# RWKV pair of a two-layer hybrid trunk: second head's products in the other two quarters of TensorE, and a new order of the work ahead

## The reference

```python
r, k, v = heads(xr @ w_rkv[0]), heads(xk @ w_rkv[1]), heads(xv @ w_rkv[2])
g = sigmoid(xg @ g1) @ g2
kk = l2_normalize(k * k_k)
logw = -softplus(-heads(w0[d] + tanh(xw @ w1[d]) @ w2[d])) - 0.5
a = sigmoid(heads(a0[d] + (xa @ a1[d]) @ a2[d]))
kd = k * (1 + (a - 1) * k_a)
# scan over tokens, context first, then latent
sa = S @ a_t
S = S * w_t + sa b_t^T + v_t k_t^T
y_t = S @ r_t
```

## Time and profile before

| | |
|---|---|
| time before, median of 3 runs | 2366.2 us (2364.81 to 2370.7) |
| the profiled execution | 2360.81 us |
| its span | 2359.0 us |
| TensorE busy | 2285.1 us, 97% |
| VectorE busy | 1561.0 us, 66% |
| ScalarE busy | 1271.2 us, 54% |
| instructions | 57897 |

### The profile page before, as it was taken

The page is one execution under the profiler, slowest core; times in us unless marked ns, Lnnn a source line. Parts: engine busy times, 40 slices in busy tenths (PEclk is TensorE's granted clock), DMA queues, the critical chain, the costliest instruction groups (busy, mean ns, idle before and its releaser), DMA issues.

```text
span 2359.0 us, 57897 instructions
## 1 busy us (share of the span) xinstructions
PE 2285.1 (97%) x25130; PEld 1898.5 (80%) x25130; DVE 1561.0 (66%) x1768; ACT 1271.2 (54%) x1407; POOL 217.8 (9%) x208
## 2 busy tenths in 40 slices
PE   8999999999999889999998899999999999999998
PEld 5677566888888478888888788888888888888886
DVE  2544785322332766556666278888888888888888
ACT  4322024322222655555554277878777878777874
POOL 2000551000000041111112020000000000000010
PEclk9999999999999999999999999999999999999999
DMA  8466225333322521111102489999999999999994
GB/s 290 183 219 246 71 80 171 89 89 97 99 89 93 166 63 60 60 60 60 51 24 65 173 323 368 373 374 370 374 367 381 361 374 370 380 360 384 357 392 172
DMA packets 228493, 512.00 MB, mean 217 GB/s; under 512 B 15271, under 2 KB 108223, under 8 KB 228031
## 3 DMA queue, kind: packets, MB, share of 16 engines
q1 hardware_dynamic: 225470, 498.61, 58.3%
q10 hardware_dynamic: 1730, 7.10, 0.9%
q0 software_dynamic: 1152, 4.19, 0.6%
HBM read 492.58 MB, written 17.30 MB: 216 GB/s over the span
## 4 chain that ended last, share of the span: by engine, by line
PE 93%; DVE 3%; issue 1%; ACT 1%; DMA 1%; POOL 0%; ACTq 0%; DVEq 0%
PE bank L1700 27%; PE bank L1730 13%; PE bank L1205 3%; PE bank L1206 3%; PE bank L1207 3%; PE bank L1332 2%; PE bank L1111 2%; PE bank L1364 2%; PE bank L1082 2%; PE bank L1083 2%; PE bank L1084 2%; PE bank L1375 2%; PE bank L1223 2%; PE bank L1222 2%; PE bank L1224 2%
## 5 line engine op out<-in xcount | busy, mean ns | idle before, releaser
L3100 DVE TENSOR_TENSOR w_low<-expert_w,w_high 128x1792 fp32r<-128x1792 f32 (+2 forms) x384 | 771.8, 2024 | 121.4 <-ACT w_high L2250 118.5
L2250 ACT CAST w_high<-expert_w 128x1792 fp32r<-128x1792 f32 (+2 forms) x384 | 652.1, 1701 | 217.2 <-PE bank L1700 144.7
L1700 PE MATMUL bank<-w_high,xg_high 128*128 128x448 f32 x1024 | 294.3, 369 | 4.2 <-DVE xg_low L3090 4.2
L1700 PE MATMUL bank<-w_low,xg_high 128*128 128x448 f32 x1024 | 293.2, 368 | 0.0
L1700 PE MATMUL bank<-w_high,xg_low 128*128 128x448 f32 x1024 | 293.1, 367 | 0.0
L1700 PEld LDWEIGHTS bank<-w_high,xg_high 128*128 128x128 f32 x1024 | 191.6, 189 | 21.6 <-DVE xg_low L3090 4.4
L1700 PEld LDWEIGHTS bank<-w_high,xg_low 128*128 128x128 f32 x1024 | 192.8, 188 | 16.9
L1700 PEld LDWEIGHTS bank<-w_low,xg_high 128*128 128x128 f32 x1024 | 193.1, 189 | 15.8
L1730 PE MATMUL bank<-w_high,hid_high 128*128 128x512 f32 x448 | 175.8, 392 | 0.0
L1730 PE MATMUL bank<-w_high,hid_low 128*128 128x512 f32 x448 | 174.9, 390 | 0.0
L1730 PE MATMUL bank<-w_low,hid_high 128*128 128x512 f32 x448 | 174.7, 390 | 0.0
(11 more groups left out here) (440 smaller groups left out, 4109.3 us busy)
## 6 DMA issues: line engine op xcount, KB each, us to landing
expert_w<-in_moe_w_dram SPq DMA_DIRECT2D x128, 1792.0 KB, 9.6
expert_w<-in_moe_w_dram SPq DMA_DIRECT2D x32, 2048.0 KB, 10.3
arena<-in_mod_w_dram SPq DMA_DIRECT2D x48, 1024.0 KB, 8.6
expert_w<-in_moe_w_dram SPq DMA_DIRECT2D x32, 1536.0 KB, 10.0
arena<-in_ffn_w_dram SPq DMA_DIRECT2D x44, 512.0 KB, 5.1
slot_rows<-arena SPq DMA_DIRECT2D x25, 512.0 KB, 5.5
arena<-in_hy_w_in_dram SPq DMA_DIRECT2D x12, 1024.0 KB, 5.3
arena<-in_rw_w_rkv_dram SPq DMA_DIRECT2D x48, 256.0 KB, 2.8
```

Source lines behind the costliest of these rows:

```text
L1700: last = pe.matmul(bank[b0 + v][:, 0:EH], x[:, k, :], w_[:, kk, v * EH:v * EH + EH], start=(k == 0 and x is XGH and w_ is wh), stop=(k == ...
L2250: act.copy(high_piece(kind, n), piece(kind, ering[q % ERN], n // 2, n % 2))\
L3100: dve.tensor_tensor(piece(kind, low[s], n // 2, n % 2), piece(kind, ering[s], n // 2, n % 2), high_piece(kind, n).bitcast(F32), ALU.subtract)\
```

## The change

- z: one step for both heads, in which for each chunk matrix head 1 uses (0,0) and (1,1) and head 2 the quarters (0,1) and (1,0).
- wu: head 2 likewise; the loop runs over d, then b, then both heads, and waits once, for both inverses. Its four sums are in banks 2d + h. The steps and copies are ordered by direction first.
- For that, head 2's matrices have their halves exchanged: `scored` writes them so (`flip`), and a is turned in pieces: per chunk matrix a transpose of 64 rows to 128 columns for head 1, and for head 2 a 64x64 product with the identity and a 64x64 transpose. ScalarE copies a by head, not by direction.
- Decay and rate of direction 0 stay ahead of wu, those of direction 1 move behind it, on TensorE and on ScalarE (behind the four copies of wu).
- VectorE adds the last level into the inverse before the bonus, not after it.
- The values of the next pair go to bank 2, from bank 6, the queries to bank 3, from bank 7. Value tile 0 stands before m, tile 1 between m and n, tile 2 behind the local output products, tiles 3 to 7 in the scan, one per state. For the pairs after the first, tiles 0 to 2 are one product of 512 columns rather than four of 128; so is the key sum.
- The local output moves into the upper halves of the banks of g (0 and 1), and `g_sum` is signalled behind it; the output projection uses banks 2, 3, 6, 7.
- PAIR_FILL becomes 4 and stands behind the queries.

```diff
-PAIR_FILL, FIRST_FILL = 3, 4
+PAIR_FILL, FIRST_FILL = 4, 4
...
-            return bank[(0, 1, 6, 7)[m // 2]][:, m % 2 * SEQ:m % 2 * SEQ + SEQ]
+            return bank[(2, 3, 6, 7)[m // 2]][:, m % 2 * SEQ:m % 2 * SEQ + SEQ]
...
-                if d == 0:
-                    fill(PAIR_FILL)
...
-                for t in range(NB):
-                    cs = slice(t * P, t * P + P)
-                    last = mm(bank[0][:, cs], heads1, KS[:, cs], start=True, stop=True)
-                last.then_inc(sem("ahead_products"), one("ahead_products", "key_sum"))
+                mm(bank[0][:, :], heads1, KS, start=True, stop=True)\
+                    .then_inc(sem("ahead_products"), one("ahead_products", "key_sum"))
...
-                    step(pe, "ahead_copies", "rate_sig_1", j)
-                    step(pe, "pair_vectors", "n_ready_1", j - 1)
+                    step(pe, "pair_copies", "wu_copy_01", j - 1)
+                    if isinstance(j, int) and j == 0:
+                        pe.wait_ge(sem("lora_taken"), 4)
                 for k in tiles:
-                    for t in range(NB):
-                        cs = slice(t * P, t * P + P)
-                        last = mm(bank[6][:, cs], wst[:, 2, k, :], XV[:, k, cs], start=(k == 0 and t == 0), stop=(k == KT - 1),
+                    width = T if j and k < 3 else P
+                    for t in range(T // width):
+                        cs = slice(t * width, t * width + width)
+                        last = mm(bank[2][:, cs], wst[:, 2, k, :], XV[:, k, cs], start=(k == 0 and t == 0), stop=(k == KT - 1),
...
                 step(pe, "pair_vectors", "g_ready_1", i - 1)
-                settle(pe)
-                scores("scored", 0, At, Bt)
                 step(pe, "pair_copies", "out_copy", i - 1)
                 settle(pe)
-                scores("keys_scored", 2, Kt, At)
+                scores("scored", 0, At, Bt, 1)
+                step(pe, "ahead_copies", "query_copy", i)
+                settle(pe)
+                scores("keys_scored", 2, Kt, At, 0)
...
-                def z(h):
-                    if h == 0:
-                        step(pe, "pair_copies", "v_copy", i)
+                def z():
+                    step(pe, "pair_copies", "v_copy", i)
                     settle(pe)
                     for x in range(2 * NB):
-                        for s_ in range(2):
-                            last = mm(bank[6 + h][hd(s_), x * C:x * C + C], AakT[h][hd(s_), x, :],
-                                      Vt[hd(s_), x % NB, hd(h)], start=True, stop=True)
-                    last.then_inc(sem("pair_products"), one("pair_products", f"z_{h}"))
+                        for h in range(2):
+                            for s_ in range(2):
+                                last = mm(bank[6 + h][hd(s_ ^ h), x * C:x * C + C], AakT[h][hd(s_), x, :],
+                                          Vt[hd(s_), x % NB, hd(h)], start=True, stop=True)
+                            if x == 2 * NB - 1:
+                                last.then_inc(sem("pair_products"), one("pair_products", f"z_{h}"))
...
-                for d in range(2):
-                    turn(2 + d, At[d]).then_inc(sem("pair_products"), one("pair_products", f"a_turned_{d}"))
+                for x in range(2 * NB):
+                    d, b = divmod(x, NB)
+                    cols, first, second = slice(x * C, x * C + C), b * P, b * P + C
+                    last = pe.transpose(bank[2][:, cols], At[d][hd(0), first:first + P], ident[hd(0), hd(0)])
+                    if x == 2 * NB - 1:
+                        last.then_inc(sem("pair_products"), one("pair_products", "a_turned_0"))
+                    mm(bank[3][hd(1), cols], At[d][hd(1), first:first + C], ident[hd(1), hd(1)], start=True, stop=True)
+                    last = pe.transpose(bank[3][hd(0), cols], At[d][hd(1), second:second + C], ident[hd(1), hd(1)])
+                last.then_inc(sem("pair_products"), one("pair_products", "a_turned_1"))
...
                 if more:
                     ahead_decay_and_rate(i + 1, 0)
+                step(pe, "pair_vectors", "inverse_1", i)
+                step(pe, "pair_copies", "z_copy_1", i)
+                settle(pe)
+                for d in range(2):
+                    for b in range(NB):
+                        for h in range(2):
+                            for r in range(2):
+                                last = mm(bank[2 * d + h][hd(r ^ h), b * P:b * P + P], TT[h][hd(r), d * NB + b, :],
+                                          Q[hd(r), 2 * h + d, b, :], start=True, stop=True)
...
+                if more:
                     ahead_decay_and_rate(i + 1, 1)
-
-                for h in range(2):
-                    step(pe, "pair_vectors", f"inverse_{h}", i)
...
+                    ahead_key_sum(i + 1)
                 if more:
-                    ahead_key_sum(i + 1)
+                    ahead_values(i + 1, range(0, 1))
                 step(pe, "pair_copies", "wu_copy_11", i)
+                if more:
+                    step(pe, "ahead_copies", "decay_sig_1", i + 1)
...
+                if more:
+                    ahead_values(i + 1, range(1, 2))
+                if more:
+                    step(pe, "ahead_copies", "rate_sig_0", i + 1)
+                    settle(pe)
...
                 if more:
-                    ahead_values(i + 1, range(0, 1))
+                    ahead_values(i + 1, range(2, 3))
                 else:
                     step(pe, "pair_finish", "pair_out", i - 1)
-                    step(pe, "pair_vectors", "g_ready_1", i)
                     out_products(0, 2)
...
-                    if more and st < 7:
-                        ahead_values(i + 1, range(st, st + 1 + (st == 6)))
+                    if more and 1 < st < 7:
+                        ahead_values(i + 1, range(st + 1, st + 2))
...
                 if more:
-                    ahead_rates(i + 1)
-                for h in range(2):
-                    for d in range(2):
+                    ahead_rates(i + 1, 0)
+                for d in range(2):
+                    for h in range(2):
                         step(act, "pair_products", f"wu_{h}{d}", i)
...
                 if more:
+                    ahead_rates(i + 1, 1)
                     ahead_key_log(i + 1)
```

More of the change, by code:

```diff
@@ L176, in _pair_steps @@
     pe += ["z_0", "z_1", "bonus_sum"]
-    pe += [f"wu_{h}{d}" for h in range(2) for d in range(2)] + ["m_sum", "n_sum", "g_sum"]
+    pe += [f"wu_{h}{d}" for d in range(2) for h in range(2)] + ["m_sum", "n_sum", "g_sum"]
     pe += [f"moved_{st}_{d}" for st in range(1, 7) for d in range(2)] + ["out_sum", "mean_sum", "var_sum"]
@@ L181, in _pair_steps @@
     act += ["v_copy", "spread_0", "spread_1", "z_copy_0", "z_copy_1"]
-    act += [f"wu_copy_{h}{d}" for h in range(2) for d in range(2)]
+    act += [f"wu_copy_{h}{d}" for d in range(2) for h in range(2)]
     act += ["out_copy", "square", "log_var", "norm"]
@@ L1345, in ahead_queries @@
                         cs = slice(t * P, t * P + P)
-                        last = mm(bank[7][:, cs], wst[:, 0, k, :], XR[:, k, cs], start=(k == 0 and t == 0), stop=(k == KT - 1),
+                        last = mm(bank[3][:, cs], wst[:, 0, k, :], XR[:, k, cs], start=(k == 0 and t == 0), stop=(k == KT - 1),
                                   skip_group_check=True)
@@ L1536, in pair @@
                                       ARR[h][r, 4 * d + c // 2, :], start=True, stop=True)
-                last.then_inc(sem("pair_products"), one("pair_products", "g_sum"))
                 for d in range(2):
@@ L2097, in ahead_values @@
                     done += one("ahead_copies", "next_high")
-                act.copy(Vf, bank[6][:, :]).then_inc(sem("ahead_copies"), done)
+                act.copy(Vf, bank[2][:, :]).then_inc(sem("ahead_copies"), done)
             def ahead_queries(j):
                 step(act, "ahead_products", "queries", j)
-                act.copy(Rf, bank[7][:, 0:SEQ]).then_inc(sem("ahead_copies"), one("ahead_copies", "query_copy"))
+                act.copy(Rf, bank[3][:, 0:SEQ]).then_inc(sem("ahead_copies"), one("ahead_copies", "query_copy"))
             def ahead_gate(j):
@@ L2131, in pair @@
                     act.copy(Btok[d], b4(4 + d)).then_inc(sem("pair_copies"), one("pair_copies", f"b_copy_{d}"))
-                for d in range(2):
-                    step(act, "pair_products", f"a_turned_{d}", i)
-                    act.copy(Q[:, d::2, :, 0:C], bank[2 + d][:, :].rearrange("p (b h c) -> p h b c", h=2, c=C))\
-                        .then_inc(sem("pair_copies"), one("pair_copies", f"a_copy_{d}"))
+                for h in range(2):
+                    step(act, "pair_products", f"a_turned_{h}", i)
+                    act.copy(Q[:, 2 * h:2 * h + 2, :, 0:C], bank[2 + h][:, :].rearrange("p (d b c) -> p d b c", d=2, c=C))\
+                        .then_inc(sem("pair_copies"), one("pair_copies", f"a_copy_{h}"))
```

(6 more changed lines are left out.)

62 lines of the change are left out of this document (29 added, 33 removed).

## The result

The changed kernel took 2388.3 us (median of 4 runs, 2385.93 to 2390.13); the kernel before, run beside it, 2365.5 (2361.29 to 2370.7). The ratio is 1.0095, 95% interval [1.0072, 1.0117]: slower by 22.8 us, where 2372.0 was forecast and the range ended at 2384. The profiled execution has a span 25.1 us longer than before.

What follows compares the result with a forecast made beforehand. TensorE, busy 97% of the span, was taken as the bound, with ScalarE and VectorE deciding what savings arrive. Seven pairs +6.7, fills +0.2, last pair -1.1 gave +5.8 us: 2372.0 us, range 2354 to 2384.

Steps and rivals of the forecast that it cites:

- z and the inverse products: z and wu on TensorE, using four quarters: z falls to about 1.0 us (saves 1.0), wu to 1.85 (saves 1.8).
- Turning a: TensorE's turn of a in mixed pieces: 17 shape changes at 0.10 us, 3.1 in all, 2.2 more than before.
- ScalarE and VectorE: Ahead of the scan: copy of a 2.15 us later, second scan 3.5 later and about 1.15 long.
- TensorE up to n: Products, value tiles and a 0.35 us issue gap ahead of the scan: n_ready 1.95 us later.
- The scan: VectorE sets the pace; one value tile less inside the scan gains 1.0 us a pair at its end.
- The last pair: No work ahead; shorter wu and removed waits outweigh the later turn: -1.1 us together.
- B: Rival: the turn of a overlaps and takes 1.05 us; -8.5 us, 2357.7; chance 0.28.
- C: Rival: TensorE's whole saving of 3.3 us a pair arrives; -24 us, 2342; chance 0.06.
- E: Rival: the parts cancel or have no effect on the pair's length; 2366 us; chance 0.05.
- D: Rival: instruction supply brings two more 1.3 us gaps in z, wu, m, n; +18 on the forecast, 2390; chance 0.06.

Runs made afterwards that it cites:

- v1_quarters: Changed kernel with a turned in 64x64 tiles throughout, so the shape changes only at the block's ends; 2407.5 us (ratio 1.0182).
- typed: Changed kernel with the turn's same 24 instructions ordered by kind, sixteen transposes first, then eight products; 2362.7 us (ratio 1.0000).
- allprod: Changed kernel with every piece of the turn an fp32 product with the identity, shapes still mixed, code length kept; 2403.5 us (ratio 1.0173).
- v2_grouped: Changed kernel with the turn's same 24 instructions ordered by shape, 64x128 transposes first, then the 64x64 instructions; 2392.1 us (ratio 1.0134).
- b_mixed: Kernel before with only the change's mixed turn of a and its copies by head, 48 more instructions a pair; 2428.4 us (ratio 1.0271).
- b_mixed2: Kernel before with the change's turn, code length kept by 512-column products for key sum and value tiles 0 to 2; 2401.7 us (ratio 1.0158).
- typed_v1late: typed with value tile 1 moved behind g and out, and tile 2 into the first state; 2362.3 us (ratio 0.9997).
- typed_v0late: typed with no value tile ahead of m and n: tile 0 behind g and out, two tiles in state 6; 2365.3 us (ratio 1.0014).
- typed_mid: typed with one value tile between m and n, none ahead of m, tile 1 behind g and out; 2358.1 us (ratio 0.9982).

## Why the prediction was wrong

The sign was right, the size not: +22.8 us measured, +5.8 forecast. In the profiled executions it was 25.1, so 19.3 were missed: 14.2 in pairs 1 to 6, of which the clock is about 6, and 6.4 in the last pair, while the first pair, what stands ahead of it and the fills came out 1.3 better. Point by point:

- **z and the inverse products**: right. 1.16 and 1.91 us for 1.0 and 1.85.
- **Turning a** is the step that failed, in size and in its reason. It priced 17 changes of shape at 0.10 us and summed to 3.1; from the first record of the block (1121.62 in the timeline) to k's first (1125.46) it took 3.84, above the upper bound of 3.6. That is some 0.8 us a pair. The bounds did not hold because the term priced the wrong thing: with no shape change it is only 0.17 us shorter (v1_quarters, with eight products more), and with a shape change at every transpose but the kinds apart 2.1 us shorter (typed). The rows for L1332 and L1308 were of products among products, where allprod confirms a cost for shape; no row that the step read was of a transpose next to a small product. The trace of before has one, though in another shape: the last 32x32 product of the levels (L1375) starts 0.18 us before b's first transpose (L1269), where these products start 0.02 us or less apart.
- **The clock behind the turn** had no term. In four pairs of the profiled run it fell to 1.2 GHz for 3.4 or 6.8 us. Pairs 3 to 6 are 62.9 us on average, pairs 1 and 2 61.4: 1.5 each, 6 in all. It goes with the long block, of alternating kinds or, in allprod, of alternating shapes: it is there in after, v2_grouped, b_mixed, b_mixed2 and allprod, and gone in typed. It does not follow each time: with a block of 3.88 us v1_quarters shows it in one of pairs 1 to 6. I had costed the block as time, not as a stretch in which TensorE gets little done. What in the block brings the clock down was not tried.
- **ScalarE and VectorE**: the mechanism was right. Against the clean pairs of before, the copy of a came 2.9 us later in pairs 1 and 2 (2.15 forecast, the rest is the turn's), the scan was 1.23 us long (1.15), and n_ready 3.2 to 3.6 later instead of 1.95. As forecast it is n on TensorE that ends last ahead of it: VectorE waited 0.5 to 1.2 us for n.
- **TensorE up to n**: right that a value tile between m and n gives the supply time. The gap there was 0.15 us in the pair shown (0.35 taken), and typed_v1late and typed_v0late show 0.8 to 1.4 where the tile is missing. But the two tiles ahead of n were counted only as delay, not as what ate the wu saving: typed_mid, with one of them fewer ahead of n, has n_ready 0.8 us earlier than typed and the whole kernel is 0.18% faster by its ratio.
- **The scan**: -0.9 a pair, as forecast (-1.0), though not because of a tile less in general: the doubled one in state 6 is gone.
- **The last pair** was to gain 1.1; with what follows it lost 5.3. Its n stood 2.49 us for instructions, a gap that I had not looked for there, and the fall of the clock behind n made two groups of products (L1559, L1409) 2.2 us longer. In the profile of v2_grouped, whose n has no gap and whose clock did not fall there, the last pair and what follows are 0.7 us shorter than before in spite of a block of 4.27.
- **Rivals**: B (everything overlaps) is refuted by the turn of 3.84 us. C is refuted too: 24 us were to be gained (and its 3.3 a pair went into the sum as 3.0). E's 2366 lies below every time of the changed kernel (from 2385.9 on). D put the danger in the supply of instructions between z and n; in pairs 1 to 6 a gap there is at most 0.17 us, and only the last pair has D's kind of gap, 2.49. So its time, 2390, was near by luck. The cited rule of the Trainium skill, page "TensorEngine Tiling (Array Packing)", section Key Properties, that a change of tiling mode drains TensorE, does not show among transposes: 64x128 and 64x64 ones on other rows begin 0.02 us apart in the turn of typed. Among fp32 products allprod (0.20 and 0.15 us at a change) agrees with it in sign.

The balance per pair, pairs without a fall of the clock: turn +3.0, z hidden, wu -1.7, two tiles ahead of n +2.1, the constant -0.9: +2.5, and the pairs are 61.4 against 58.95. It is good to some 0.5 us: of the turn's 3.0 about 2.4 reach wu in pair 2, and n is 0.4 longer. Stays open: why alternating kinds cost 0.13 us each time, what brings the clock down, and on what number or boundary the supply of instructions hangs.

## What to carry to other kernels

Order small TensorE work by kind: put transposes together and fp32 products together, and look at the clock behind any stretch of small work that has become longer. Before crediting a saving, find the one point on which the period hangs (here n_ready, plus a constant) and ask what stands ahead of it and what could stand behind it at no cost. Keep the number of instructions in a loop unchanged in experiments, or the experiment measures that instead.

## What was not expected of the hardware

- A transpose next to an fp32 product of a 64-row tile: 0.13 us at each change, 16 times a pair; transposes of either shape one after the other 0.03 us each (sixteen in 0.49 us).
- Sixteen semaphore increments a pair on TensorE's queue: +47.4 us, through gaps of 0.76 and 2.23 us in other places of the pair and the lower clock near them.
- Products that use two quarters at a time, changing to the other two after every eight, took 2.6 us where two quarters throughout took 3.64 and four in turn 1.91. Around each change their records start 0.04 to 0.06 us apart instead of 0.10: groups overlap there.
- The version that beats both, typed_mid: 2358.1 us, 3.8 below the kernel before beside it, an interval of 0.1 to 0.3%.
